# A gated recurrence in steps of one block instead of two, with the operands kept in five buffers instead of four

## What is computed

```
def rg_lru(x, gx_w, gx_b, ga_w, ga_b, lru_lambda):
    xb = x.reshape(B, S, LRU_BLOCKS, LRU_BLOCK_DIM)
    gate_i = jax.nn.sigmoid(jnp.einsum("bsnd,nde->bsne", xb, gx_w) + gx_b)...
    gate_r = jax.nn.sigmoid(jnp.einsum("bsnd,nde->bsne", xb, ga_w) + ga_b)...
    log_a = -LRU_C * jax.nn.softplus(-lru_lambda) * gate_r
    a = jnp.exp(log_a)
    mult = jnp.sqrt(-jnp.expm1(2.0 * log_a))
    u = mult * gate_i * x
    ... h[t] = a[t] * h[t-1] + u[t], over the tokens
```

## Time and profile before

| | us |
|---|---|
| median of three runs | 3431.4 (3431.08 to 3432.77) |
| the profiled execution's own time | 3432.28 |
| its span, first to last instruction | 3430.5 |
| TensorE busy | 3341.5 (97%) |
| VectorE busy | 1638.5 (48%) |
| ScalarE busy | 1291.4 (38%) |
| GpSimd busy | 515.0 (15%) |

### The profile page before, as it was taken

How to read it: one execution, slowest core, us unless ns; L and a number is a source line. 1 busy time by engine, 2 the same in 40 slices (tenths; PEclk the granted TensorE clock), 3 DMA queues, 4 the chain that set the end, 5 groups by cost and what they waited for, 6 DMA issues and landing times.

```text
span 3430.5 us, 41764 instructions
## 1 busy us (share of the span) xinstructions
PE 3341.5 (97%) x16431; PEld 2700.0 (79%) x16431; DVE 1638.5 (48%) x2695; ACT 1291.4 (38%) x2000; POOL 515.0 (15%) x749
## 2 busy tenths in 40 slices
PE   7999999999999999999999899999999999999998
PEld 6777887887888888888888676788878888777886
DVE  7895655344343454444343556553424343355443
ACT  4443433343233333433342436532323323355432
POOL 0001312322110000110330011021000111110211
PEclk9999999999999999999999999999999999999999
DMA  6776433546348776544335343363433643433642
GB/s 211 216 231 199 132 105 105 154 145 208 132 160 227 210 215 184 173 159 141 123 111 170 119 129 102 122 214 119 147 88 111 200 151 117 132 111 102 208 148 92
DMA packets 279523, 525.06 MB, mean 153 GB/s; under 512 B 64189, under 2 KB 99588, under 8 KB 274720
## 3 DMA queue, kind: packets, MB, share of 16 engines
q1 hardware_dynamic: 223504, 340.79, 33.0%
q0 software_dynamic: 53648, 178.32, 15.2%
q10 hardware_dynamic: 2176, 3.28, 0.4%
HBM read 408.32 MB, written 113.97 MB: 152 GB/s over the span
## 4 chain that ended last, share of the span: by engine, by line
PE 73%; DVE 3%; ACT 3%; issue 2%; DMA 1%; POOL 0%; ACTq 0%; POOLq 0%; DVEq 0%
PE pg L631 64%; PE pm L1322 2%; PE pm L1351 2%; PE pm L1338 1%; PE pm L2426 1%; ACT whi L390 1%; DMA mx_g<-zt 1%; PE pm L2430 0%; PE pm L2414 0%; DVE r_y L1707 0%; DVE d_x L2514 0%; PE pm L2405 0%; ACT stage L501 0%; PE pm L1819 0%; ACT w_p L1387 0%
## 5 line engine op out<-in xcount | busy, mean ns | idle before, releaser
L396 DVE TENSOR_TENSOR wlo<-raw,whi 128x1024 fp32r<-128x1024 f32 x523 | 663.2, 1273 | 1251.5 <-ACT whi L390 1250.5
L390 ACT ACTIVATE whi<-raw 128x1024 fp32r<-128x1024 f32 x523 | 548.7, 1054 | 1100.3 <-PE pg L631 1090.2
L631 PE MATMUL pg<-a_hi,whi 128*128 128x512 f32 x1856 | 743.9, 401 | 11.4 <-DVE wlo L396 4.8
L631 PE MATMUL pg<-a_hi,wlo 128*128 128x512 f32 x1856 | 726.7, 392 | 0.0
L631 PE MATMUL pg<-a_lo,whi 128*128 128x512 f32 x1856 | 726.2, 391 | 0.0
L631 PE MATMUL pg<-b_hi,whi 128*128 128x512 f32 x1568 | 620.8, 396 | 8.7 <-DVE stage L572 3.2
L631 PE MATMUL pg<-b_hi,wlo 128*128 128x512 f32 x1568 | 612.2, 390 | 0.0
L631 PE MATMUL pg<-b_lo,whi 128*128 128x512 f32 x1568 | 611.5, 390 | 0.0
L631 PEld LDWEIGHTS pg<-a_hi,whi 128*128 128x128 f32 x1856 | 348.4, 188 | 90.7 <-issue 14.2
L631 PEld LDWEIGHTS pg<-a_hi,wlo 128*128 128x128 f32 x1856 | 348.1, 188 | 77.5
L631 PEld LDWEIGHTS pg<-a_lo,whi 128*128 128x128 f32 x1856 | 348.7, 188 | 73.6 <-issue 2.6
(11 more groups left out here) (442 smaller groups left out, 3843.7 us busy)
## 6 DMA issues: line engine op xcount, KB each, us to landing
raw<-in_l_w_in SPq DMA_DIRECT2D x169, 512.0 KB, 3.7
raw<-in_ab_w_in SPq DMA_DIRECT2D x112, 512.0 KB, 3.7
zt<-stage POOLq DMA_DIRECT2D x142, 256.0 KB, 3.6
raw<-in_c_w_in SPq DMA_DIRECT2D x64, 512.0 KB, 4.9
raw<-in_l_w_out SPq DMA_DIRECT2D x64, 512.0 KB, 3.9
raw<-in_ab_w_out SPq DMA_DIRECT2D x32, 512.0 KB, 3.8
raw<-in_glu_w SPq DMA_DIRECT2D x32, 512.0 KB, 4.2
raw<-in_c_w_out SPq DMA_DIRECT2D x32, 512.0 KB, 3.7
```

The costliest lines, as they stand in the source:

```text
L390: nc.scalar.activation(used(whi, n), used(raw, n), ACT.Copy).then_inc(hi_ready, 1)
L396: nc.vector.tensor_tensor(used(wlo, n), used(raw, n), used(whi, n).bitcast(F32), ALU.subtract).then_inc(lo_ready, 1)
L631: ins = nc.tensor.matmul(pg[m][:r.rows(m), :r.cols()], lhsT, rhs, start=(kt == 0 and n_pass == 0), stop=(kt == r.kts - 1 and n_pass == 2))
```

## The change

`LRU_STEPS` becomes 12 and a step takes one block. In step s VectorE convolves block s, forms the root's input of block s - 2 (and `r_i` times `r_y`), and finishes and scans block s - 4; ScalarE takes the root of block s - 3, then the gates, exponential and tanh of block s; TensorE multiplies block s; GpSimd loads block s + 1 and stores block s - 5 (the last two in the last step). The buffers of `r_y`, `r_i`, `r_r` and `r_a` become five. ScalarE's first sigmoid is now that to `r_r`. The leads of TensorE and ScalarE become 5; those of VectorE and GpSimd stay 3.

```
+    LRU_SLOTS = 5
...
-    LRU_STEPS = RB // 2 + 1
+    LRU_STEPS = RB + 4
...
+        for step in range(LRU_STEPS):
+            if 0 < step < RB - 1:
+                load(step + 1)
+            for n in (range(step - 5, step - 4) if step < LRU_STEPS - 1 else (RB - 2, RB - 1)):
...
+        for step in range(LRU_STEPS):
+            root, n = step - 3, step
+            if 0 <= root < RB:
+                act.wait_ge(ru_m, root + 1)
+                nc.scalar.activation(at("r_r", root), at("r_r", root), ACT.Sqrt).then_inc(ru_q, 1)
+            if n < RB:
                 act.wait_ge(ru_g, n + 1)
+                if n >= LRU_SLOTS:
+                    act.wait_ge(ru_o, n - LRU_SLOTS + 1)
+                nc.scalar.activation(at("r_r", n), pm[2 * (n % 2) + 1][:, :], ACT.Sigmoid, bias=col("ga_b", n)).then_inc(ru_s, 1)
+                nc.scalar.activation(at("r_i", n), pm[2 * (n % 2)][:, :], ACT.Sigmoid, bias=col("gx_b", n)).then_inc(ru_s, 1)
+                act.wait_ge(ru_s, 2 * n + 2)
                 act.wait_ge(ru_sp, 1)
+                nc.scalar.activation(at("r_a", n), at("r_r", n), ACT.Exp, scale=sp[:, 4, n:n + 1]).then_inc(ru_a, 1)
+                act.wait_ge(ru_a, 2 * n + 1)
+                nc.scalar.activation(at("r_r", n), at("r_r", n), ACT.Tanh, scale=sp[:, 5, n:n + 1]).then_inc(ru_a, 1)
...
+        for step in range(LRU_STEPS):
+            if step < RB:
+                convolved(step)
+            if 0 <= step - 2 < RB:
+                gain_squared(step - 2)
+            if 0 <= step - 4 < RB:
+                scanned(step - 4)
             yield
...
-        beside(lru_pe(pe), LRU_STEPS, pe, pe_piece, SWA_IN, 3)
+        beside(lru_pe(pe), LRU_STEPS, pe, pe_piece, SWA_IN, 5)
...
-        beside(lru_act(act), LRU_STEPS, act, act_piece, SWA_IN, 3)
+        beside(lru_act(act), LRU_STEPS, act, act_piece, SWA_IN, 5)
```

More of the change, by code:

```diff
@@ L1584, in build @@
         loads=(fox_loads, 64), values=fox_values, units0=0, jobs0=0, tiles0=0, in0=0, sink=None, lam=None, gain=None)
+    LRU_SLOTS = 5
     V2 = overlay(0, [
-        ("r_x", [2, L + CW - 1], F32), ("r_y", [4, L], F32), ("r_i", [4, L], F32),
-        ("r_r", [4, L], F32), ("r_a", [4, L], F32), ("r_m", [2, L], F32),
+        ("r_x", [2, L + CW - 1], F32), ("r_y", [LRU_SLOTS, L], F32), ("r_i", [LRU_SLOTS, L], F32),
+        ("r_r", [LRU_SLOTS, L], F32), ("r_a", [LRU_SLOTS, L], F32), ("r_m", [2, L], F32),
         ("r_o", [2, L], F32), ("r_gx", [RB, P], F32), ("r_ga", [RB, P], F32)])
@@ L1612, in lru_pool @@
         pool.dma_start(V2["r_ga"][:, :, :], inp["l0_gate_a_w_2"].rearrange("n d e -> d n e")).then_inc(shared_in, 16)
[L1613 to L1617, removed]
+        for step in range(LRU_STEPS):
+            if 0 < step < RB - 1:
+                load(step + 1)
+            for n in (range(step - 5, step - 4) if step < LRU_STEPS - 1 else (RB - 2, RB - 1)):
+                if n >= 0:
                     pool.wait_ge(ru_o, n + 1)
@@ L1624, in lru_pe @@
         pe.wait_ge(shared_in, 80)
-        for pair in range(RB // 2 + 1):
-            for n in range(2 * pair, min(2 * pair + 2, RB)):
+        for n in range(LRU_STEPS):
+            if n < RB:
                 pe.wait_ge(ru_y, n + 1)
@@ L1629, in lru_pe @@
                     pe.wait_ge(ru_s, 2 * (n - 1))
-                nc.tensor.matmul(pm[2 * (n % 2)][:, :], V2["r_gx"][:, n, :], V2["r_y"][:, n % 4, :], start=True, stop=True)
-                nc.tensor.matmul(pm[2 * (n % 2) + 1][:, :], V2["r_ga"][:, n, :], V2["r_y"][:, n % 4, :],
+                nc.tensor.matmul(pm[2 * (n % 2)][:, :], V2["r_gx"][:, n, :], V2["r_y"][:, n % LRU_SLOTS, :], start=True, stop=True)
+                nc.tensor.matmul(pm[2 * (n % 2) + 1][:, :], V2["r_ga"][:, n, :], V2["r_y"][:, n % LRU_SLOTS, :],
                                  start=True, stop=True).then_inc(ru_g, 1)
@@ L1641, in lru_act @@
         sp = r_sp
[L1642 to L1648, removed]
-                act.wait_ge(ru_g, n + 1)
[L1650 to L1656, removed]
-                act.wait_ge(ru_sp, 1)
[L1658 to L1665, removed]
@@ new lines, in lru_act @@
+        at = lambda name, n: V2[name][:, n % LRU_SLOTS, :]
+        for step in range(LRU_STEPS):
[3 more added lines that the diff above has]
+                nc.scalar.activation(at("r_r", root), at("r_r", root), ACT.Sqrt).then_inc(ru_q, 1)
+            if n < RB:
+                act.wait_ge(ru_g, n + 1)
+                if n >= LRU_SLOTS:
[3 more added lines that the diff above has]
+                act.wait_ge(ru_s, 2 * n + 2)
+                act.wait_ge(ru_sp, 1)
+                nc.scalar.activation(at("r_a", n), at("r_r", n), ACT.Exp, scale=sp[:, 4, n:n + 1]).then_inc(ru_a, 1)
+                act.wait_ge(ru_a, 2 * n + 1)
+                nc.scalar.activation(at("r_r", n), at("r_r", n), ACT.Tanh, scale=sp[:, 5, n:n + 1]).then_inc(ru_a, 1)
@@ L1694, in lru_dve @@
             vec.memset(V2["r_x"][:, n, :CW - 1], 0.0).then_inc(ru_e, 1)
[L1695 to L1728, removed]
@@ new lines, in lru_dve, with convolved @@
+        at = lambda name, n: V2[name][:, n % LRU_SLOTS, :]
+        def convolved(n):
+            s = n % 2
+            dve.wait_ge(ru_in[s], 16 * (n // 2 + 1))
+            if n >= LRU_SLOTS:
+                dve.wait_ge(ru_g, n - LRU_SLOTS + 1)
+                dve.wait_ge(ru_o, n - LRU_SLOTS + 1)
+            x, y = V2["r_x"][:, s, :], at("r_y", n)
+            tap = lambda i: col("conv_w", i * RB + n)
+            run(vec.tensor_scalar(y, x[:, 0:L], tap(0), col("conv_b", n), ALU.mult, ALU.add))
+            for i in range(1, CW):
+                ins = vec.scalar_tensor_tensor(out=y, in0=x[:, i:i + L], scalar=tap(i), in1=y, op0=ALU.mult, op1=ALU.add)
+                run(ins) if i < CW - 1 else ins.then_inc(ru_y, 1)
+            dve.wait_ge(ru_y, n + 1)
@@ new lines, in gain_squared, with scanned @@
+        def gain_squared(n):
+            dve.wait_ge(ru_a, 2 * n + 2)
+            run(vec.tensor_tensor(V2["r_m"][:, n % 2, :], at("r_a", n), at("r_a", n), ALU.mult))
+            vec.scalar_tensor_tensor(out=at("r_r", n), in0=V2["r_m"][:, n % 2, :], scalar=1.0, in1=at("r_r", n), op0=ALU.add,
+                                     op1=ALU.mult).then_inc(ru_m, 1)
+            run(vec.tensor_tensor(at("r_i", n), at("r_i", n), at("r_y", n), ALU.mult))
+        def scanned(n):
+            dve.wait_ge(ru_q, n + 1)
+            run(vec.tensor_tensor(at("r_i", n), at("r_i", n), at("r_r", n), ALU.mult))
+            if n >= 2:
+                dve.wait_ge(mix_out[n % 2], tile_stored(1, n - 2))
+            vec.tensor_tensor_scan(V2["r_o"][:, n % 2, :], at("r_a", n), at("r_i", n), 0.0, ALU.mult, ALU.add).then_inc(ru_o, 1)
```

## The result

| | before | changed |
|---|---|---|
| median | 3431.08 (five runs, 3429.24 to 3432.77) | 3411.47 (five runs, 3409.54 to 3417.23) |
| again, beside other kernels | 3431.15 | 3412.43 (3411.22 to 3415.01) |
| profiled execution: time, span | 3432.28, 3430.5 | 3409.54, 3407.7 |
| stretch from the end of `SWA_IN`'s piece 2 to the attention's first matmul | 152.2 | 137.7 |

The ratio is 0.9948 (95% interval 0.9933 to 0.9962), so the change makes the kernel faster by 0.4 to 0.7%. The forecast was 3419 with a range of 3413 to 3427. Direction and mechanism were right, the size was short by a third. The two traced executions differ by 22.8 us: 2.6 ahead of the stretch, 14.5 in it, 5.6 behind it.

What follows compares the result with a forecast made beforehand. TensorE was taken to bound the recurrence's stretch, losing 24.2 us there. Lost time -14.4 (24.2 to 9.8, edges included) and clock +2.4 gave -12.0, so 3431.4 became 3419 us, range 3413 to 3427.

Steps and rivals of the forecast that it cites:

- The wait for the gates' weights (-8.2): Ahead of block 0: TensorE's wait of 6.1 us and its slow stretch of 2.1 go, -8.2.
- The walk: Queues stepped through with traced durations: TensorE waits 2.0 at piece 8's bank 0, 1.9 at block 5, 0.4 at convolution 6, 1.5 before piece 16.
- signs of being wrong: ScalarE without idle between blocks 3 and 7, `r_y` waits before most blocks, clock not above 0.94, or a later stretch growing.
- The edges of fp32 groups (+2.4): On TensorE in the recurrence: eight one-block groups cost 4.0 us at their edges instead of 1.6, +2.4.
- The clock behind the new waits (+2.4): Slow matmuls behind TensorE's three waits of 1.5 to 2.0 us: between 0 and 4.8, half taken, +2.4.
- Rival B: TensorE's waits vanish or stay under 1 us as VectorE reaches scalings and convolution 5 earlier: about -19, 3412; chance 0.06.
- Rival C: Added ScalarE latency is paid by TensorE in each step from 3 to 7, waits lower the clock: -6, 3425; chance 0.16.
- Rival E: Slower: the loop of block, gates, copy, split and convolution outlasts TensorE's step, every block waits: +9, 3441; chance 0.08.

Runs made afterwards that it cites:

- twelve steps without leads: The changed kernel with the leads of TensorE and ScalarE back at 3, twelve steps and five buffers kept: ratio 0.9999 to the kernel before.
- pairs with leads 4, 4, 2: The kernel before, steps of two blocks kept, with leads of TensorE and ScalarE 4 and VectorE 2: 3407.5 us, again 3407.9.
- pairs with leads 5, 5, 3: The kernel before, steps of two blocks kept, with leads of TensorE and ScalarE 5 instead of 3, VectorE still 3: 3417.7 us, ratio 0.9962.
- two kernels with added loads: The changed kernel with one, or two, more ScalarE table loads ahead of each block's wait for its gates: 3418.2 and 3422.7 us.

## Why the prediction was right, and where it was short

- **The wait for the gates' weights (-8.2).** Right: the idle 5.95 us and the low clock behind it are gone, and the leads alone bring it.
- **The walk.** Waits of 2.0, 1.9, 0.4 and 1.5 were predicted and 2.09, 2.04, none and 1.16 measured, each at the place and for the reason named. The first fp32 matmul came at 1894.02 instead of 1896.6, since TensorE was 2.6 us early already ahead of the stretch. One figure of the working has no source: VectorE's 8.5 us a step were set against 9.7 of TensorE's, but the 17.05 us for two steps make 8.5; the waits didn't rest on it. Of the signs of being wrong one came near: ScalarE had no idle time around block 4, but 2.53 us ahead of block 5's gates and 1.67 ahead of block 7's. The same walk gave the waits of six other orders mostly to some tenths of a us (4.46 for 4.3, 1.10 for 0.8, 1.67 for 1.4, 4.61 for 4.5; at the worst 2.65 for 2.0), except that it overstated the chain of small waits in the twelve steps without leads.
- **The edges of fp32 groups (+2.4): wrong.** I had charged 0.4 us whenever a piece's matmuls follow an fp32 group, because the first one takes 0.63 to the next. In the changed kernel a block takes 1894.02 to 1895.97 with its first matmul of a piece, 1.95 us, and 4 x 0.43 + 0.227 is 1.95: the last fp32 record is short by what the next one is long. The 4.0 us for eight groups don't exist. In the total of the kernel before it did no harm, since that was taken from the measured 152.3; it only moved 1.6 us from the clock's account to the edges'.
- **The clock behind the new waits (+2.4): short.** Two of the three waits had a slow stretch, of 1.7 us each, 3.4 together. With the waits at 5.8 from start to start and 0.1 behind the third, that makes 9.3 of the 9.6 us that the stretch of 137.7 has above 128.1. In total the prediction had -12.0 for the stretch and -14.5 was measured.
- **Outside the stretch.** The prediction put nothing here. The medians moved by 19 to 20 us, the stretch by 14.5, and by the granted clock the other 5 are low clock. A place at half clock behind the stretch costs some 1.7 us, half of the 3.4 of the row above (one, in the second trace of the pairs with leads 4, 4, 2, is twice as long). Without these places the part behind the stretch is 1371.7 and 1373.1 us in the kernel before, 1372.9 and 1372.3 in the changed one, and 1371.4 to 1374.2 in all twelve traces.
- **It is not the chance of two traces.** The granted clock and the span of each execution give an estimate of what low clock costs it in all, (1 - clock) x span. That is 31 us in the kernel before (mean of 36 executions) and 22 in the changed kernel (eleven), 9 less, of which the stretch has 3.4 to 5.1. The pairs with leads 5, 5, 3 lose 24.5, and there the stretch has nearly all of the difference. It fits that, with each kernel's stretch taken from its median time, 3274 to 3275 us are left for the changed kernel, 3279 for those pairs and 3279 to 3281 for the kernel before (the other orders lie at 3275 to 3279). Why the clock falls less often outside the stretch in the changed kernel stays open. The waits ahead of those places are the same (1.8, 2.1 and 1.4 us) but for the one at the banks of the latent keys' product (`lk_hi`): 2.15 and 2.46 before, 1.67 and 1.50 in the changed kernel, 2.82 and 3.55 in the pairs with leads 4, 4, 2.
- **Rival B** (3412) has the nearest time, but for another reason: the waits did not vanish. **Rival C** has the sensitivity right, but not the places: the two kernels with added loads show that ScalarE's time is paid by TensorE, at block 5 and piece 16 and, with two loads, a little at piece 8, not in each step. **Rival E** would have needed still more than 2.57 us a block; at that the kernel is still 10 us faster than the kernel before beside it (3422.7 and 3433.1). The 1.28 us of a load next to the activation before it (1933.98 + 0.63, then 1934.63) hold again, with no drain beside them. In the Trainium skill, page "ScalarE: Activation LUTs", section "What ACT_TABLE_LOAD costs", a drain of 1.38 is added to each switch; these rows don't agree. What its rule to finish one set first would be worth here, no run shows by itself.
- **What I did not ask** is which part of the change does it. I had given the leads 8.2 of the 14.4 us and the finer steps the rest. By the runs the leads alone give 13.8 of 14.5, the finer steps alone lose 1.6, and on top of these leads they give 0.7. By the medians of the same round they give 5.3 there (3417.7 and 3412.4); by the estimate above nearly all of the rest is low clock outside the stretch.

## What to carry to other kernels

Where engines run programs that are interleaved by hand, what counted here is which foreign instruction stands ahead of the one that is waited for, more than how fine the steps are: write down for each handover what is queued ahead of it, and try first the numbers that shift one engine's program against another's. Three such numbers gave 0.7% here, slightly more than a new schedule with two of these numbers moved, a fifth buffer and ten more table loads. A walk through the queues, with the durations of one trace, found the waits to some tenths of a us; a comparison of one stretch between traces, bounded by events on the engine that sets the time, resolves 0.2 us where whole runs resolve 3.

## What the runs showed of the hardware that was not expected

- An idle stretch of TensorE of 1.4 to 2.6 us may or may not be followed by matmuls at half speed: 2.57 with and without (kernel before, twelve steps with no lead moved), 2.14 at the same place with and without. When it is (granted clock 0.50), it costs some 1.7 us in most places here. I could not tell ahead which.
- The switch from fp32 matmuls to the rounded ones costs nothing (a block and the first matmul of a piece take 1.95 us, 4 x 0.43 + 0.227), though the first record behind it is 0.4 us longer: the last fp32 record is shorter by the same.
- Added table loads on ScalarE that nobody needs cost 1.28 us each on that engine and start 0.01 to 0.02 us after what is ahead of them.
